# Gate projection of a hybrid attention block: six tiles cut into two pieces of four k-tiles each

## The chip, the cores and the metric

The program runs on one core of one Trainium2 chip. The metric is the device time of one execution, in microseconds (us). The chip's engines are named as in the profile: PE is TensorE's matrix multiply and PEld its weight load, DVE is VectorE, ACT is ScalarE, POOL is GpSimd, SP is SyncE, whose queue issues the DMAs.

## The reference, cut to what matters

One decoder layer is computed for 512 positions and a width of 1024: three attention branches, a gated merge, and a SwiGLU channel mixer. The change touches the gates (`z_a`, the first of three) while branch B, the differential attention, is being computed:

```python
h = rmsnorm(x, g_norm1[l]) * (1 + sc1) + sh1
(a_q, ..., b_q, b_k, b_v, ..., z_a, z_b, z_c) = split_cols(h @ w_in[l], IN_SPLITS)
# branch B, per block of 128 queries and per head:
logits = jnp.einsum('bqhmd,bshmd->bmhqs', qb, k) * ATTN_SCALE + bias
p = jax.nn.softmax(logits, axis=-1)
attn = (p[:, 0] - lam * p[:, 1]).astype(v.dtype)
out = jnp.einsum('bhqs,bshe->bqhe', attn, v)
o_b = rmsnorm(o_b, g_subln[l]) * (1 - lam_init)
merged = (jax.nn.sigmoid(z_a) * (o_a @ w_branch_a[l])
          + jax.nn.sigmoid(z_b) * (o_b @ w_branch_b[l])
          + jax.nn.sigmoid(z_c) * (o_c @ w_branch_c[l]))
```

## The kernel before

Every large projection is computed in split precision: the input and the weights are each cut into a high and a low part, and a k-tile (128 of the 1024 input channels) costs three matmuls of 128x512: high by high (line 846), low by high (847), high by low (848). One output tile of a projection has eight k-tiles and is gathered in one of two PSUM banks, `tile_ps`. Weights come in chunks of 256 columns: SP loads `w_raw` by DMA, ACT rounds it into `w_hi` (line 1419), and DVE subtracts to get `w_lo` (`make_lo`, line 1805). There are two buffers of each.

The middle of the program is a table of steps v = 0 to 87, written out by hand; each engine walks through it in its own fixed order. Steps 64 to 79 are branch B's sixteen (head, block) pairs. Step v has the width 128 x (v mod 4 + 1), so 79 has 512 columns and 76 has 128. The steps 80 to 87 only drain what the sixteen began. Beside the attention work a step can hold a dense piece: a few k-tiles of a projection that has nothing to do with the attention of this step. `dense_at(v)` says which. In this part of the table it is the gate projection: six tiles z0 to z5, from the weight chunks 20 (z0, z1), 21 (z2, z3) and 22 (z4, z5).

In step v of branch B the engines do, each in this order:

- PE: the scores of v, two maps (line 1097), where each map needs the bank that DVE's shift of step v-1 has read; the dense piece, if any; the transposes of the probabilities of v-2 (line 1112), which need DVE's mix of v-2; the products with the values of v-3 (line 1144), which need ACT's copy of the transposes; in steps 73, 77, 81 and 85 the transposes of one head's normed output (line 1175, called the head transposes here), which need DVE's scaling.
- DVE: shift of the first map (add the bias table, take the maximum, line 2014); reciprocal of the sums of v-1 (line 2040), which needs ACT's exponentials; shift of the second map; mix of v-1 (line 2048, first map minus lambda times second), which needs POOL's normalising; then `make_lo` of a weight chunk if `lo_at(v)` names one; then, in steps 71, 75, 79 and 83, one small addition on the mean squares (line 2109); in steps 72, 76, 80 and 84 the scaling of a head's output (line 2119, four blocks); in steps 73, 77, 81 and 85 the low part of it (line 2025).
- ACT: two exponentials (line 1564), a weight chunk's high part if one is due (line 1419), the eviction of a z tile that this step ends (line 1426), the copy of the transposed probabilities (line 1576), and after products that end a head four squares (line 1639).
- POOL: normalising of the second map of v-1 (line 783), then, in steps 71, 75 and 79, the power -1/2 of one head's mean squares (line 729); that of the last head follows step 80.

After step 87 PE goes on at once with the branch A product (`oa_hi`, `oa_lo`; also lines 846 to 848), which needs chunk 23.

The pieces of a z tile have 3, 3 and 2 k-tiles, in three consecutive steps:

```python
Z_STEPS = (66, 69, 72, 76, 80, 84)
for n, v0 in enumerate(Z_STEPS):
    if v0 <= v < v0 + 3:
        return ("z", n), (range(0, 3), range(3, 6), range(6, 8))[v - v0]
```

`chunk_starting_at` names the step in which PE first uses a chunk; ACT makes the high part of the following chunk one step later. `lo_at` names the step in which DVE makes a chunk's low part.

Of the kernel before, what the change touches and what calls it, by code (L numbers as in the profile page):

```python
# [61 lines left out]
MIX_C1, MIX_A, MIX_B, N_MIX = 16, 32, 64, 80  # L62
# [2 lines left out]
SUM_W = 100  # L65
N_DIRECT = (2, 1)
OC_STEPS = (49, 57)
Z_STEPS = (66, 69, 72, 76, 80, 84)
NL_RING, NLB_RING = 4, 7


# [60 lines left out]
def dense_at(v):  # L132

    if v < MIX_A:
        return ("bqk", v // 4), range(2 * (v % 4), 2 * (v % 4) + 2)
    n, part = divmod(v - MIX_A - 2, 4)
    if 0 <= n < 8 and part < 3:
        return ("bv", n), (range(0, 3), range(3, 6), range(6, 8))[part]
    for n, v0 in enumerate(Z_STEPS):
        if v0 <= v < v0 + 3:  # L140
            return ("z", n), (range(0, 3), range(3, 6), range(6, 8))[v - v0]
    return None


def dense_ending_at(v):

    d = dense_at(v)
    return d[0] if d is not None and KT - 1 in d[1] else None


def chunk_starting_at(v):

    return {0: 14, 8: 15, 16: 16, 24: 17, MIX_A + 2: 18, MIX_A + 18: 19, Z_STEPS[0]: 20, Z_STEPS[2]: 21,
            Z_STEPS[4]: 22}.get(v)


def lo_at(v):

    return {2: 15, 10: 16, 18: 17, 26: 18, MIX_A + 5: 19, MIX_A + 21: 20, Z_STEPS[0] + 2: 21, Z_STEPS[2] + 4: 22,
            Z_STEPS[4] + 2: 23}.get(v)  # L160


def attention_tiles():

    names = []
    for v in range(N_STEP):
        if len(qlat_at(v)) == 1:
            names.append(("qlat", qlat_at(v)[0]))
        if dense_at(v) is not None and 0 in dense_at(v)[1]:
            names.append(dense_at(v)[0])  # L170
        for p in products_at(v):
            if uv_after(p) is not None:
                names.append(("uv", uv_after(p)))
        if len(qlat_at(v)) == 2:
            names += [("qlat", h) for h in qlat_at(v)]
        if v in OC_STEPS:
            names.append(("oc", OC_STEPS.index(v)))
        if ob_at(v) is not None:
            names.append(("ob", ob_at(v)))
    return {n: TL_ATT + t for t, n in enumerate(names)}  # L180
# [30 lines left out]
def hybrid_block(nc, a, out):  # L211
# [10 lines left out]
    with ctx:  # L222
# [600 lines left out]
        def _(pe):  # L823
# [354 lines left out]
            def project_z(v):  # L1178

                if chunk_starting_at(v) is not None:  # L1180
                    chunk_ready(chunk_starting_at(v))
                (_, n), kts = dense_at(v)
                project((CH_Z + n // 2) % 2, ATT_TILE["z", n], h_hi, h_lo, [(k, k) for k in kts], n % 2 * P,
                        first=0 in kts, last=KT - 1 in kts)

            def project_b(v):

                if chunk_starting_at(v) is not None:
                    chunk_ready(chunk_starting_at(v))
                (kind, n), kts = dense_at(v)  # L1190
                t = ATT_TILE[kind, n]
                if kind == "bqk":
                    project((CH_BQK + n // 2) % 2, t, h_hi, h_lo, [(k, k) for k in kts], n % 2 * P,
                            first=0 in kts, last=KT - 1 in kts)
                    return
                s, r = (CH_BV + n // 4) % 2, n % 4
                b = tile_start(t) if 0 in kts else t % 2
                for kt in kts:
                    hh, hl = h_hi[:, kt, r * P:(r + 1) * P], h_lo[:, kt, r * P:(r + 1) * P]
                    pe.matmul(tile_ps[b][:, 0:CW], hh, w_hi[s][:, kt, :], start=kt == 0, stop=False)  # L1200
                    pe.matmul(tile_ps[b][:, 0:CW], hh, w_lo[s][:, kt, :], start=False, stop=False)
                    mm = pe.matmul(tile_ps[b][:, 0:CW], hl, w_hi[s][:, kt, :], start=False, stop=kt == KT - 1)
                if KT - 1 in kts:
                    mm.then_inc(tile_made[b], 1)
# [584 lines left out]
        def _(dve):  # L1789
# [239 lines left out]
            for v in range(N_STEP):  # L2029
                if v < N_MIX:  # L2030
                    shift(subs_of(v)[0])
                if v < MIX_B and lo_at(v) is not None:
                    make_lo(lo_at(v))
# [16 lines left out]
                if v >= MIX_B and lo_at(v) is not None:  # L2050
                    make_lo(lo_at(v), kt=4 if lo_at(v) == chunk_z(0) + 3 else KT)
# [346 lines left out]
```

## Time and profile before

| | |
|---|---|
| median of 3 runs | 1005.82 us (1005.34 to 1005.87) |
| profiled execution | 1006.29 us |
| its span, first to last instruction | 1004.5 us |
| PE busy | 987.5 us, 98% of the span |
| DVE busy | 481.5 us, 48% |
| ACT busy | 380.8 us, 38% |
| POOL busy | 98.5 us, 10% |
| granted TensorE clock, mean | 0.999 of full speed |

The profiled execution is 1.8 us longer than its span, which covers what lies before the first and after the last instruction. A timeline row gives the start and the duration of an instruction in us, its engine, line, operation, and what it writes and reads; in brackets stands how long the engine was idle before it and who released it. On PE the ends are modelled and overlap the following instruction, so the distance from one start to the next tells what an instruction costs. A granted clock of 1.00 is the upper of TensorE's two levels, 2.4 GHz.

### The profile page before, as it was taken

What the parts mean: (1) busy time and instruction counts of PE and PEld (TensorE: products, weight loads), DVE (VectorE), ACT (ScalarE), POOL (GpSimd) and SP (SyncE); (2) the same over time, 40 slices, a digit from 0 to 9 for tenths busy, and PEclk for the clock granted to TensorE, in tenths of its full rate; (3) what the DMA queues carried; (4) which work ended last, traced back from release to release, by engine and by line L of the source; (5) the groups of instructions that cost most, each with busy time, mean ns of one, the idle gap of its engine ahead of it and who ended that gap; (6) DMA issues with size and microseconds to landing.
All of it is one profiled execution on the core that took longest, in us unless ns stands there. A gap on an engine that the chain in (4) does not pass through costs nothing.

```text
span 1004.5 us, 12705 instructions
## 1 busy us (share of the span) xinstructions
PE 987.5 (98%) x4925; PEld 805.2 (80%) x4925; DVE 481.5 (48%) x827; ACT 380.8 (38%) x679; POOL 98.5 (10%) x137
## 2 busy tenths in 40 slices
PE   7999999999999999999999999999999999999997
PEld 5778888878877777788788888988888888788886
DVE  4654777833245335663745563743433343331324
ACT  5345422255566666543232232442322322221222
POOL 1500000000054522200000002000000000000401
PEclk9999999999999999999999999999999999999999
DMA  8884226312230201155455642123344434232312
GB/s 330 254 267 143 85 84 177 95 43 84 63 108 22 74 22 33 53 193 195 158 192 198 220 175 84 63 84 104 104 136 151 131 104 147 84 105 84 126 43 84
DMA packets 88164, 123.13 MB, mean 123 GB/s; under 512 B 4825, under 2 KB 69942, under 8 KB 87987
## 3 DMA queue, kind: packets, MB, share of 16 engines
q1 hardware_dynamic: 87442, 115.98, 35.3%
q0 software_dynamic: 528, 6.22, 2.1%
q8 instruction: 32, 0.52, 0.2%
q10 hardware_dynamic: 144, 0.26, 0.1%
q14 instruction: 18, 0.14, 0.0%
HBM read 119.77 MB, written 8.45 MB: 128 GB/s over the span
## 4 chain that ended last, share of the span: by engine, by line
PE 91%; DMA 3%; DVE 2%; ACT 1%; issue 1%; POOL 1%; SPq 0%; POOLq 0%; DVEq 0%; ACTq 0%
PE tile_ps L846 18%; PE tile_ps L848 18%; PE tile_ps L847 18%; DMA w_raw<-in_w_in_dram 2%; PE t_ps L1112 2%; PE s_ps L1094 2%; PE o_ps L1141 2%; PE tile_ps L1295 1%; PE s_ps L1295 1%; PE s_ps L1293 1%; PE t_ps L1295 1%; PE t_ps L1293 1%; PE tile_ps L1294 1%; PE tile_ps L1293 1%; PE s_ps L1294 1%
## 5 line engine op out<-in xcount | busy, mean ns | idle before, releaser
L846 PE MATMUL tile_ps<-h_hi,w_hi 128*128 128x512 f32 x736 | 292.6, 398 | 1.4 <-DVE w_lo L1805 0.8
L848 PE MATMUL tile_ps<-h_hi,w_lo 128*128 128x512 f32 x736 | 287.1, 390 | 0.0
L847 PE MATMUL tile_ps<-h_lo,w_hi 128*128 128x512 f32 x736 | 286.8, 390 | 0.0
L1805 DVE TENSOR_TENSOR w_lo<-w_raw,w_hi 128x2048 fp32r<-128x2048 f32 (+3 forms) x60 | 131.0, 2183 | 161.2 <-ACT w_hi L1419 161.2
L846 PEld LDWEIGHTS tile_ps<-h_hi,w_hi 128*128 128x128 f32 x736 | 138.2, 188 | 38.1 <-issue 8.2
L848 PEld LDWEIGHTS tile_ps<-h_hi,w_lo 128*128 128x128 f32 x736 | 138.1, 188 | 29.3
L847 PEld LDWEIGHTS tile_ps<-h_lo,w_hi 128*128 128x128 f32 x736 | 138.3, 188 | 26.9 <-issue 0.2
L1419 ACT ACTIVATE w_hi<-w_raw 128x2048 fp32r<-128x2048 f32 (+3 forms) x60 | 107.3, 1789 | 42.6 <-DMA w_raw<-in_w_in_dram 10.9
L1802 DVE TENSOR_TENSOR t_lo<-t_raw,t_hi 128x2048 fp32r<-128x2048 f32 (+1 forms) x15 | 32.8, 2183 | 85.6 <-ACT t_hi L1417 85.5
L1564 ACT ACTIVATE nl<-nl,cst 128x256 f32<-128x256 f32 (+3 forms) x81 | 43.0, 531 | 49.3 <-DVE cst L2014 49.2
L1417 ACT ACTIVATE t_hi<-t_raw 128x2048 fp32r<-128x2048 f32 (+1 forms) x15 | 27.0, 1799 | 81.5 <-PE s_ps L1295 53.5
L1752 ACT ACTIVATE f_hi<-f_t 128x512 f32 (+1 forms) x22 | 13.9, 633 | 88.3 <-DVE f_t L2305 88.3
L1576 ACT ACTIVATE pt<-t_ps 128x128 f32<-128x128 f32 (+2 forms) x80 | 32.2, 402 | 28.9 <-PE t_ps L1112 28.2
L769 POOL TENSOR_TENSOR tm<-tab,score 128x256 f32<-128x256 f32 (+2 forms) x24 | 24.3, 1014 | 175.1 <-DVE cst L2014 175.1
L1746 ACT ACTIVATE silu_t<-tile_ps 128x512 f32<-128x512 f32 x22 | 13.0, 597 | 72.0 <-PE tile_ps L848 71.9
L2305 DVE TENSOR_TENSOR f_t<-tile_ps,silu_t 128x512 f32<-128x512 f32 x20 | 13.8, 692 | 54.7 <-PE tile_ps L848 54.7
L804 POOL TENSOR_TENSOR x<-gated,x 128x512 f32<-128x512 f32 x4 | 5.0, 1287 | 297.2 <-DVE gated L2226 297.2
L1112 PEld LDWEIGHTS t_ps<-ident,nl 128*128 128x128 f32 x160 | 20.2, 140 | 12.1 <-issue 4.3
L1112 PE MATMUL t_ps<-ident,nl 128*128 128x128 f32 x160 | 29.6, 275 | 0.0
L2144 DVE SCALAR_TENSOR_TENSOR ada_sum<-ada,cst,ada_sum 128x1024 f32<-128x1024 f32 x21 | 26.9, 1283 | 0.7
L1968 DVE MATCH_REPLACE8 score<-cst,score 128x256 f32<-128x256 f32 (+2 forms) x48 | 26.0, 548 | 0.0
L1960 DVE MAX8 cst<-score 128x8 f32<-128x256 f32 (+2 forms) x48 | 25.2, 556 | 1.4
(404 smaller groups left out, 1679.4 us busy)
## 6 DMA issues: line engine op xcount, KB each, us to landing
w_raw<-in_w_in_dram SPq DMA_DIRECT2D x31, 1024.0 KB, 5.5
w_raw<-in_w_gate_up_dram SPq DMA_DIRECT2D x22, 1024.0 KB, 6.9
ada<-in_w_ada_dram SPq DMA_DIRECT2D x12, 1024.0 KB, 5.5
t_raw<-in_w_down_dram SPq DMA_DIRECT2D x10, 1024.0 KB, 5.0
row_copies<-row_flat POOLq DMA_DIRECT2D x1, 5632.0 KB, 21.6
ada<-in_w_ada_dram SPq DMA_DIRECT2D x8, 640.0 KB, 11.5
ada<-in_w_ada_dram SPq DMA_DIRECT2D x8, 512.0 KB, 4.2
ada<-in_w_ada_dram SPq DMA_DIRECT2D x8, 384.0 KB, 9.9
```

The costliest lines, as they stand in the source:

```text
L846: pe.matmul(dst[0:mw, :], wh, x_hi[:, kx, :], start=start, stop=False)
L847: pe.matmul(dst[0:mw, :], wh, x_lo[:, kx, :], start=False, stop=False)
L848: mm = pe.matmul(dst[0:mw, :], wl, x_hi[:, kx, :], start=False, stop=stop)
L1112: mm = pe.transpose(t_ps[v % 2][:, j * P:(j + 1) * P], src[:, j * P:(j + 1) * P], ident[:])
L1293: pe.matmul(bank[:], x_hi[:, kx, blk], wh[:, kw, :], start=start, stop=False)
L1295: mm = pe.matmul(bank[:], x_lo[:, kx, blk], wh[:, kw, :], start=False, stop=stop)
L1417: act.activation(t_hi[s][:, 0:wide, :], t_raw[s][:, 0:wide, :], ACT.Copy).then_inc(w_hi_made[s], 1)
L1419: hi = nc.scalar.activation(w_hi[s][:, 0:kt, 0:n_cols], w_raw[s][:, 0:kt, 0:n_cols], ACT.Copy)
L1564: act.activation(b, b, ACT.Exp, bias=negmax[:, k:k + 1], scale=-1.0, accum_out=expsum[:, k:k + 1]).then_inc(exped, 1)
L1576: act.activation(pt[v % 2][:, 0:w], t_ps[v % 2][:, 0:w], ACT.Copy).then_inc(pt_ready, 1)
L1802: dve.tensor_tensor(t_lo[s][:, 0:wide, :], t_raw[s][:, 0:wide, :], t_hi[s][:, 0:wide, :].bitcast(F32), ALU.subtract).then_inc(w_split[s], 1)
L1805: dve.tensor_tensor(w_lo[s][:, 0:kt, 0:n_cols], w_raw[s][:, 0:kt, 0:n_cols], w_hi[s][:, 0:kt, 0:n_cols].bitcast(F32), ALU.subtract) \
```

## The change

The six z tiles are cut into two pieces of four k-tiles, and the steps that hold them are written out. Low parts of chunk 22 and 23 are made in steps 75 and 80, where it was 76 and 82.

```diff
-Z_STEPS = (66, 69, 72, 76, 80, 84)
+Z_STEPS = ((66, 67), (69, 70), (71, 73), (74, 75), (78, 79), (82, 83))
@@ dense_at
-    for n, v0 in enumerate(Z_STEPS):
-        if v0 <= v < v0 + 3:
-            return ("z", n), (range(0, 3), range(3, 6), range(6, 8))[v - v0]
+    for n, steps in enumerate(Z_STEPS):
+        if v in steps:
+            part = steps.index(v)
+            return ("z", n), range(4 * part, 4 * part + 4)
@@ chunk_starting_at
-    return {0: 14, 8: 15, 16: 16, 24: 17, MIX_A + 2: 18, MIX_A + 18: 19, Z_STEPS[0]: 20, Z_STEPS[2]: 21,
-            Z_STEPS[4]: 22}.get(v)
+    return {0: 14, 8: 15, 16: 16, 24: 17, MIX_A + 2: 18, MIX_A + 18: 19, Z_STEPS[0][0]: 20, Z_STEPS[2][0]: 21,
+            Z_STEPS[4][0]: 22}.get(v)
@@ lo_at
-    return {2: 15, 10: 16, 18: 17, 26: 18, MIX_A + 5: 19, MIX_A + 21: 20, Z_STEPS[0] + 2: 21, Z_STEPS[2] + 4: 22,
-            Z_STEPS[4] + 2: 23}.get(v)
+    return {2: 15, 10: 16, 18: 17, 26: 18, MIX_A + 5: 19, MIX_A + 21: 20, 68: 21, 75: 22, 80: 23}.get(v)
```

Before, every step from 66 to 86 except 75, 79 and 83 held a piece. After, the steps 68, 72, 76, 77, 80, 81, 84, 85 and 86 hold none; 71, 73, 75, 79 and 83 hold four k-tiles. No engine has more or fewer instructions: 3164 rows on PE, 672 on DVE, 438 on ACT, with POOL and SP unchanged in order too.

On PE, in steps 75 to 77 (scores with `s_ps<-bqk`, transposes with `t_ps<-ident`, products with `o_ps<-bv`), the order was this, with the remaining k-tiles of a piece left out:

```order
L1097 MATMUL s_ps<-bqk 128x512 x2
L1112 MATMUL t_ps<-ident,nl_112 128x128 x2
L1144 MATMUL o_ps<-bv,pt_116 128x128
L1097 MATMUL s_ps<-bqk 128x128 x2
L846 MATMUL tile_ps<-h_hi,w_hi_54 128x512
...
L1112 MATMUL t_ps<-ident,nl_114 128x128 x3
L1144 MATMUL o_ps<-bv,pt_117 128x128 x2
L1097 MATMUL s_ps<-bqk 128x256 x2
```

It is now this, up to the transposes of step 77:

```order
L1097 MATMUL s_ps<-bqk 128x512 x2
L846 MATMUL tile_ps<-h_hi,w_hi_54 128x512
...
L1112 MATMUL t_ps<-ident,nl_112 128x128 x2
L1144 MATMUL o_ps<-bv,pt_116 128x128
L1097 MATMUL s_ps<-bqk 128x128 x2
L1112 MATMUL t_ps<-ident,nl_114 128x128 x3
L1144 MATMUL o_ps<-bv,pt_117 128x128 x2
L1097 MATMUL s_ps<-bqk 128x256 x2
L1112 MATMUL t_ps<-ident,nlb_137 128x128 x4
```

The piece moved from behind the scores of 76 to behind those of 75, and the transposes of 75 (`nlb_137`) now follow the scores of 77 directly, where a piece of three k-tiles stood between them.

On DVE, in the steps 75 and 76, the low part of chunk 22 (`w_lo_55`) passed the small addition, both shifts and the mix of step 75:

```order
 L2048 SCALAR_TENSOR_TENSOR nl_114<-nl_114,cst,nlb_136 128x384
+L1805 TENSOR_TENSOR w_lo_55<-w_raw_51,w_hi_53 128x2048
 L2109 TENSOR_SCALAR cst<-cst 128x4
 L2014 ISA nl_111,cst<-s_ps,tab_129 128x128
...
 L2048 SCALAR_TENSOR_TENSOR nlb_137<-nlb_137,cst,nlb_138 128x512
-L1805 TENSOR_TENSOR w_lo_55<-w_raw_51,w_hi_53 128x2048
 L2119 TENSOR_SCALAR olat<-o_ps,cst 128x128 x4
```

It stands now ahead of the small addition that POOL's power waits for, and ahead of the mix of 75.

On DVE, in step 80, the low part of chunk 23 (`w_lo_56`, half a chunk) moved ahead of the scaling of the third head:

```order
 L2048 SCALAR_TENSOR_TENSOR nlb_138<-nlb_138,cst,nl_111 128x512
+L1805 TENSOR_TENSOR w_lo_56<-w_raw_52,w_hi_54 128x1024
 L2119 TENSOR_SCALAR olat<-o_ps,cst 128x128 x4
 L2025 SCALAR_TENSOR_TENSOR ob_lo<-tile_ps,cst,ob_hi 128x512
-L1805 TENSOR_TENSOR w_lo_56<-w_raw_52,w_hi_54 128x1024
```

The scaling, for which the head transposes of step 81 wait, now comes behind it.

## Rows read from the trace of the kernel before

**Rows 1.** The page, part 1: busy us, share of the span, instructions.

```profile
PE 987.5 (98%) x4925; PEld 805.2 (80%) x4925; DVE 481.5 (48%) x827; ACT 380.8 (38%) x679; POOL 98.5 (10%) x137
```

**Rows 2.** Windows, steps 64 to 87: length, busy us by engine, clock, DMA.

```profile
358.00:429.30 71.30, 70.76 (x389) 52.38 (x388) 38.23 (x126) 42.94 (x134) 14.48 (x21) 1.00 0.15 45
```

**Rows 3.** Timeline of PE: z0's first piece of three k-tiles, step 66.

```profile
365.22 0.50 PE L846 MATMUL tile_ps<-h_hi,w_hi 128*128 128x512 f32 x1
365.55 0.40 PE L847 MATMUL tile_ps<-h_lo,w_hi 128*128 128x512 f32 x1
...
366.02 0.40 PE L846 MATMUL tile_ps<-h_hi,w_hi 128*128 128x512 f32 x1
...
367.39 0.27 PE L1112 MATMUL t_ps<-ident,nlb 128*128 128x128 f32 x1
```

**Rows 4.** Timeline of PE: steps 68 and 69.

```profile
373.85 0.50 PE L846 MATMUL tile_ps<-h_hi,w_hi 128*128 128x512 f32 x1
...
375.35 0.49 PE L1112 MATMUL t_ps<-ident,nl 128*128 128x128 f32 x3
...
376.21 0.70 PE L1097 MATMUL s_ps<-bqk 64*128 64x256 f32 x4
377.08 0.50 PE L846 MATMUL tile_ps<-h_hi,w_hi 128*128 128x512 f32 x1 [0.16 <-ACT z L1426]
```

**Rows 5.** Timeline of DVE: shift of step 68's first map.

```profile
375.33 0.29 DVE L2014 CUSTOM_DVE_ANT_0 nlb<-s_ps,tab 128x128 f32<-128x128 f32 x1
```

**Rows 6.** Timeline of ACT: eviction of z0, and the copy behind it.

```profile
376.45 0.57 ACT L1426 ACTIVATE z<-tile_ps 128x512 f32<-128x512 f32 x1
376.93 0.47 ACT L1576 ACTIVATE pt<-t_ps 128x384 f32<-128x384 f32 x1
```

**Rows 7.** Timeline of PE: steps 75 to 77.

```profile
399.02 1.13 PE L1097 MATMUL s_ps<-bqk 64*128 64x512 f32 x4
...
400.93 0.48 PE L1097 MATMUL s_ps<-bqk 64*128 64x128 f32 x2 [0.19 <-DVE cst L2014]
401.60 0.48 PE L1097 MATMUL s_ps<-bqk 64*128 64x128 f32 x2 [0.19 <-DVE cst L2014]
402.02 0.50 PE L846 MATMUL tile_ps<-h_hi,w_hi 128*128 128x512 f32 x1
...
407.87 0.60 PE L1112 MATMUL t_ps<-ident,nlb 128*128 128x128 f32 x4
```

**Rows 8.** Timeline of DVE: steps 75 and 76.

```profile
402.28 0.17 DVE L2109 TENSOR_SCALAR cst<-cst 128x4 f32<-128x4 f32 x1
...
404.35 0.75 DVE L2048 SCALAR_TENSOR_TENSOR nlb<-nlb,cst,nlb 128x512 f32<-128x512 f32 x1 [1.43 <-POOL nlb L783]
405.02 2.28 DVE L1805 TENSOR_TENSOR w_lo<-w_raw,w_hi 128x2048 fp32r<-128x2048 f32 x1
407.22 1.12 DVE L2119 TENSOR_SCALAR olat<-o_ps,cst 128x128 f32<-128x128 f32 x4
```

**Rows 9.** Timeline of PE: scores of step 79, head transposes of step 81.

```profile
412.97 1.13 PE L1097 MATMUL s_ps<-bqk 64*128 64x512 f32 x4
...
420.59 0.60 PE L1175 MATMUL tile_ps<-ident,olat 128*128 128x128 f32 x4
```

**Rows 10.** Timeline of DVE: scalings of two heads, low part of chunk 23.

```profile
418.98 1.12 DVE L2119 TENSOR_SCALAR olat<-o_ps,cst 128x128 f32<-128x128 f32 x4
...
422.62 1.22 DVE L1805 TENSOR_TENSOR w_lo<-w_raw,w_hi 128x1024 fp32r<-128x1024 f32 x1
...
425.99 1.13 DVE L2119 TENSOR_SCALAR olat<-o_ps,cst 128x128 f32<-128x128 f32 x4 [1.14 <-POOL cst L729]
```

**Rows 11.** Timeline of PE: the last products of branch B, step 82.

```profile
422.42 1.05 PE L1144 MATMUL o_ps<-bv,pt 128*128 128x128 f32 x8
423.27 0.50 PE L846 MATMUL tile_ps<-h_hi,w_hi 128*128 128x512 f32 x1
```

**Rows 12.** Windows at the end of the program, columns as in rows 2.

```profile
998.00:1000.00 2.00, 0.16 (x2) 0.00 (x0) 0.85 (x2) 0.51 (x2) 0.19 (x1) 1.00 0.36 136
1000.00:1002.00 2.00, 0.00 (x0) 0.00 (x0) 0.75 (x1) 0.72 (x1) 0.55 (x1) 1.00 0.00 0
```

## The prediction

> **What bounds the kernel now.** I read the page first: PE is busy for 987.5 us of 1004.5 [rows 1], and nothing else passes half. The program is PE's instructions laid end to end, so the time changes only by what PE pays between them and by what PE waits for. Then I read the windows around the change: in the 71.3 us of steps 64 to 87 PE is busy for 70.76 us [rows 2], so there is hardly a stall to win back, and any stall that the new order brings is added to the end. The list of waits agrees: PE waits in three places of that stretch [rows 4, 7]. Last I followed the timelines of PE, DVE, ACT and POOL step by step. The reader should see there that a step's probabilities travel from PE over DVE, ACT, POOL and DVE back to PE, and that the dense pieces are the work under which PE hides this way. The change takes that cover from some steps and doubles it up in others; PE's total is the same.
>
> **What a piece costs.** The first matmul of a piece is followed after 0.33 us, every other one after about 0.23 [rows 3]: a piece has a start price of 0.10 us. Two further k-tiles take 367.39 - 366.02 = 1.37 us, so 0.69 each; a piece of three is 2.17 us and one of four 2.17 + 0.69 = 2.86 us. Eighteen pieces become twelve. Two of the six starts saved stood behind scores, four behind products or transposes, where the price is much the same; four steps now go from scores straight to transposes, for which I charge 0.05 us each, half the start price, as the transposes also follow the odd-shaped score matmuls. Sum: -6 x 0.10 + 4 x 0.05 = -0.4 us. The bounds are -0.6 (no charge) and -0.2 (the full one).
>
> The Trainium skill bears on that price ("TensorE: Matmul & The Clock Gate", section "Step-by-step: what each phase is for"): it says that PE pulls a weight load ahead of matmuls in flight when row groups don't conflict or when the load goes to the background buffer. By that, a start would cost nothing and the term would be zero, 0.4 us slower than my sum. The trace shows the 0.10 us, so the row decides.
>
> **Waits that go.** In step 69 PE waits for z0's bank: from the scores to z1 it is 377.08 - 376.21 = 0.87 us where those scores alone take 0.63, the 0.70 of the row less its overlap of 0.07 [rows 4], so 0.24 us. z0 will end two steps ahead of z1, and this goes. In step 76 the two score matmuls each wait for a shift of step 75, because step 75 has no piece: 0.19 us, and then 402.02 - 400.93 = 1.09 us for work of 0.42 (from 401.60 to 402.02), so 0.19 + 0.67 = 0.86 us [rows 7]. Step 75 gets a piece, and this goes too. Together -1.1 us.
>
> **Waits that come.** There are four, each the difference between a chain and PE's own work over the same stretch.
>
> - Step 69. It now waits for DVE's first shift of step 68, since step 68 has no piece. That shift ends at 375.62 before [rows 5]. Step 66's longer piece delays all by 0.69, and z0's eviction, now in step 67, takes 0.48 us on ACT [rows 6] ahead of a copy and of the high part of branch A's last head, for which DVE waits ahead of that shift. So 375.62 + 0.69 + 0.48 + 0.06 for the signal = 376.85. PE's work would bring it there at 376.21 + 0.69 + 0.69 for the two longer pieces, - 1.50 for the piece of step 68 (373.85 to 375.35), + 0.05 = 376.14 [rows 4]. Wait: 0.7 us.
> - Step 77. The transposes of step 75 wait for its mix. From the scores of 75 to DVE's small addition it is 402.28 - 399.02 = 3.26 us [rows 7, 8]. The low part of chunk 22, 2.20 us from start to start, now stands before that addition. From the addition over POOL's power and normalising to the end of the mix it is 405.10 - 402.28 = 2.82 us. With 0.05 for the signal the chain is 8.33 us long. PE's own work before was 407.87 - 399.02 = 8.85 us; less the 0.86 of waits, less two pieces of three (4.34), plus one of four (2.86), it is 6.5 us. Wait: 1.8 us. Step 76's and 77's scores are queued ahead and are not late for it; the head transposes of step 77 and everything behind are.
> - Step 80 and 81. From the scores of 79 to the scaling of the third head it is 418.98 - 412.97 = 6.01 us [rows 9, 10]. The half chunk 23, 1.22 less the 0.08 by which DVE's instructions overlap, now stands ahead of it, and the scaling itself takes 1.12: 6.01 + 1.14 + 1.12 + 0.05 = 8.3 us until the head transposes may start. PE's work there was 420.59 - 412.97 = 7.62 us with two pieces of three; with one of four it is 7.62 - 4.34 + 2.86 = 6.15. Wait: 2.2 us, in up to three portions (transposes of 79 and a copy by ACT come late on the way, inside that sum).
> - Step 85. From the start of the last products to the end of the fourth head's scaling it is 427.12 - 422.42 = 4.70 us, over ACT's squares, DVE, POOL and DVE [rows 10, 11]. Two pieces of z5 (six k-tiles) covered it; now the products take 0.85 and one piece 2.86, 3.71 in all. Wait: 4.75 - 3.71 = 1.0 us.
>
> The sum is 0.7 + 1.8 + 2.2 + 1.0 = 5.7 us that come, -1.1 that go, -0.4 for starts: **+4.2 us**.
>
> **What costs nothing.** The evictions of z2 to z4 move by a step or two; they are under 0.6 us on ACT [rows 6], and between a tile's end and the next tile in that bank PE has at least the transposes, products and scores of a step. The high parts of chunks 22 and 23 are made one and two steps earlier, still steps ahead of their low parts. The DMA queue only waits on DVE's low parts and shifts in this stretch, and chunk 24 is asked for once the low part of 22 is made, a dozen steps before its use. After step 87 PE continues with 24 matmuls of the branch A product on chunk 23, 24 x 0.23 = 5.5 us, which is ready long before. Under it lie ACT's and DVE's work for the next tiles, as before; z5's eviction comes off that stretch, which gives at most 0.05 us. Later stages are paced by PE, which waits for nothing there, so the delay reaches the end unchanged.
>
> **How the sum stands.** On the profiled execution it gives a span of 1008.7 and 1010.5 us in all; this execution is 0.47 us over the median of the runs. On the median: 1005.82 + 4.2 = 1010.0 us.
>
> **The rivals.**
>
> - *The chains are shorter than charged.* Each was put together from distances that contain waits of DVE for PE, for example that DVE reached the addition of step 75 late since step 74's and 75's shifts came close together. If DVE runs further ahead, the two middle waits are halved: 2.0 us less, 1008.0. Against: the scores that start both chains are the trigger in any order, and what follows them has no slack in the rows. 8%.
> - *The cover was not needed* (the other side). If the transposes and head transposes find their data in time, as they do in every step of the trace now, only the terms with a minus stay: 1005.8 - 1.5 = 1004.3 us. The deciding point is whether the four waits together stay under 1.5 us. For it: none of the four waits exists in the trace. Against: for each the chain is over the cover by 0.7 to 2.2 us. 5%, within 0.2% of before; going beyond that, 2%, would need a saving in the starts of over twice the row.
> - *The clock falls.* The pauses bring PE's activity down around steps 76 to 81. If the granted clock fell to 1.2 GHz for the length of one piece, 2.86 us would double: 1012.9 us. Against: at the end of the program PE has hardly worked from 998 to 1002 us and the granted clock in these rows is still 1.00, that is 2.4 GHz [rows 12]. 4%. The Trainium skill ("TensorE: Matmul & The Clock Gate", section "What's actually happening") says that the clock's default is the throttled level and that it goes back there when PE is idle; the rows show a longer idle stretch without a fall, so the page does not change the sum.
> - *The change doesn't do what it says.* The order on each engine excludes this: the pieces stand where the table puts them.
>
> **How the numbers follow.** The forecast has 81%. Its own range, from +2.8 (every wait 0.3 smaller) to +5.2 (each 0.2 larger, starts at -0.2), is 1008.6 to 1011.0. Down to 1007.6 the range takes in the first rival; the upper end is 1011.2. What is left out is the second rival, the clock, and tails. A measurement of this kernel tells 0.2% (2.0 us) from no change. Slower by more: the forecast, the clock, and half of the first rival, 0.88 with tails. Within: the other half and the second rival, 0.10. Faster: 0.02.
>
> **What would show it.** PE's busy time in the stretch should stay and its length grow by 4 us. The list of waits should have PE waiting for the mix (line 2048) before the transposes of step 75, for the scaling (line 2119) before the head transposes of steps 81 and 85, and for a shift (line 2014) before the scores of 69; the waits for z and in step 76 should be gone. If the low part of chunk 22 is not between the mix of 74 and the addition in time, or the gaps sum to under 3 us, the chains were misjudged; if matmul distances rise above 0.23 us, it is the clock.

## The result, and the profile after

The changed kernel takes 1012.66 us in the median of 4 runs (1011.89 to 1013.77), the kernel before 1005.85 us; the ratio is 1.0063 with a 95% interval of 1.005 to 1.0075. It is slower, as forecast, but by 6.8 us where 4.2 were forecast, and outside the range, whose upper end was 1011.2. The profiled execution took 1011.89 us, with a span of 1009.7.

The page, part 1, of the changed kernel; [rows 1] is the same line of before:

```profile
PE 988.9 (98%) x4925; PEld 805.8 (80%) x4925; DVE 481.5 (48%) x827; ACT 381.6 (38%) x679; POOL 99.0 (10%) x137
```

PE's busy time has grown by 1.4 us although it runs the same 4925 instructions. That is a first sign that something else than waiting was added.

The start of the program differs from execution to execution (z0's first matmul begins at 365.22 us before, at 363.67 after, with nothing changed ahead of it), so I compare one stretch in all runs: from the first matmul of z0 to the first of the branch A product, called **the stretch** below. It is read from one profiled execution of each kernel. It was 429.32 - 365.22 = 64.10 us long and is 434.14 - 363.67 = 70.47 us now, 6.37 more. In windows of exactly these bounds (length, busy us by engine, clock, DMA), the kernel before:

```profile
365.22:429.32 64.10, 63.56 (x343) 47.58 (x343) 35.88 (x114) 38.33 (x119) 13.35 (x19) 1.00 0.15 46
```

and the changed one:

```profile
363.67:434.14 70.47, 65.70 (x344) 49.17 (x343) 35.34 (x113) 39.01 (x119) 13.41 (x19) 0.98 0.14 42
```

PE stands still for 4.8 us of it instead of 0.5, is busy for 2.1 us more (65.70 against 63.56), and the granted clock is 0.98 on average instead of 1.00. The waits, in the timeline of PE of the changed kernel; the two waits of [rows 7] and the one of [rows 4] are gone:

```profile
375.30 0.97 PE L1097 MATMUL s_ps<-bqk 64*128 64x256 f32 x4 [0.65 <-DVE cst L2014]
...
409.14 0.99 PE L1112 MATMUL t_ps<-ident,nlb 128*128 128x128 f32 x4 [1.49 <-DVE nlb L2048]
...
422.43 0.71 PE L1144 MATMUL o_ps<-bv,pt 128*128 128x128 f32 x4 [0.33 <-ACT pt L1576]
...
423.42 0.66 PE L1112 MATMUL t_ps<-ident,nlb 128*128 128x128 f32 x4 [0.27 <-DVE nlb L2048]
...
425.68 0.63 PE L1175 MATMUL tile_ps<-ident,olat 128*128 128x128 f32 x4 [0.94 <-DVE olat L2119]
...
433.75 0.63 PE L1175 MATMUL tile_ps<-ident,olat 128*128 128x128 f32 x4 [1.06 <-DVE olat L2119]
```

They stand at the four places that the prediction named: the scores of step 69, the transposes of 75, the steps 80 and 81, the head transposes of 85. What it had put at 4% is there too. The windows of two microseconds around the second wait, same columns; the third number from the end is the clock:

```profile
406.00:408.00 2.00, 1.62 (x10) 1.03 (x8) 0.90 (x7) 1.25 (x5) 1.49 (x2) 1.00 0.15 35
408.00:410.00 2.00, 0.85 (x5) 0.86 (x6) 1.66 (x5) 0.00 (x0) 0.30 (x1) 0.83 1.02 358
410.00:412.00 2.00, 2.00 (x11) 1.86 (x10) 1.22 (x7) 1.50 (x5) 0.45 (x1) 0.50 0.00 0
412.00:414.00 2.00, 2.00 (x9) 1.13 (x8) 0.97 (x2) 0.76 (x2) 0.00 (x0) 0.82 0.00 0
```

0.50 is the lower of TensorE's levels, 1.2 GHz. PE had worked on small matmuls since 404.7 us and waited for 1.5 us up to 409.14. The clock fell when PE was already at work again: a mean of 0.83 over 2 us is 0.68 us at the lower level, so since 409.3. By the 0.82 of the last window it was back at about 412.7. Under the lowered clock lay most of the transposes of 75 (the row of 409.14 above) and, behind them, the products and head transposes of step 77 and the scores of 78:

```profile
409.93 1.49 PE L1144 MATMUL o_ps<-bv,pt 128*128 128x128 f32 x6
411.21 1.06 PE L1175 MATMUL tile_ps<-ident,olat 128*128 128x128 f32 x4
412.20 1.16 PE L1097 MATMUL s_ps<-bqk 64*128 64x384 f32 x4
413.29 0.50 PE L846 MATMUL tile_ps<-h_hi,w_hi 128*128 128x512 f32 x1
```

That is 4.15 us from the transposes (409.14) to the piece (413.29). The same instructions took from 407.87 [rows 7] to 410.35 in the kernel before, 2.48 us. By these rows the lowered clock cost 1.7 us.

### The profile page after: what moved, and what is told of

It reads as the page before. It is cut to its first block, busy times and chain, and to the rows that moved or that the text cites. A ratio compares the mean times of both kernels' runs of the same rounds, so it can differ in the third digit from the quotient of the medians.

```text
span 1009.7 us, 12705 instructions
## 1 busy us (share of the span) xinstructions
PE 988.9 (98%) x4925; PEld 805.8 (80%) x4925; DVE 481.5 (48%) x827; ACT 381.6 (38%) x679; POOL 99.0 (10%) x137
## 4 chain that ended last, share of the span: by engine, by line
PE 90%; DMA 3%; DVE 2%; issue 2%; ACT 1%; POOL 1%; SPq 0%; POOLq 0%; DVEq 0%; ACTq 0%
PE tile_ps L846 18%; PE tile_ps L848 18%; PE tile_ps L847 17%; DMA w_raw<-in_w_in_dram 2%; PE t_ps L1112 2%; PE s_ps L1094 2%; PE o_ps L1141 2%; PE tile_ps L1294 1%; PE tile_ps L1293 1%; PE s_ps L1294 1%; PE s_ps L1293 1%; PE t_ps L1294 1%; PE t_ps L1293 1%; PE tile_ps L1295 1%; PE s_ps L1295 1%
```

## The experiments

Ten kernels were run. All stretches stand in one table, with what was forecast for each. "Clock falls" is about the stretch. Each ratio is to runs of the kernel before on the same chip, whose medians were 1005.85 us for the changed kernel, 1006.37 for the edits of one place and the six fill matmuls, 1005.94 for the two runs that take the change apart ("both low parts"), and 1006.03 for the rest.

| run | stretch, us | forecast | clock falls | median, us | ratio (95%) |
|---|---|---|---|---|---|
| before | 64.10 | | no | 1005.85 | |
| changed | 70.47 | 68.3 | yes | 1012.66 | 1.0063 (1.005 to 1.0075) |
| low part of 22 in step 73 | 67.70 | 67.5 | no | 1010.31 | 1.004 (1.0026 to 1.0054) |
| six fill matmuls in step 77 | 68.93 | 68.8 | no | 1011.13 | 1.0047 (1.003 to 1.0063) |
| three fill matmuls | 68.88 | 68.9 | no | 1012.36, one run | |
| low part of 23 in step 82 | 69.33 | 69.4 | yes | 1011.21 | 1.006 (1.0036 to 1.0084) |
| z5 in steps 83, 84 | 69.18 | 69.4 | yes | 1012.15 | 1.0061 (1.0044 to 1.0078) |
| the three edits at once | 65.25 | 65.5 | no | 1007.36 | 1.0012 (1.0003 to 1.0022) |
| changed, both low parts back | 70.28 | 70.1 | yes | 1012.43 | 1.0062 (1.0045 to 1.0079) |
| before, both low parts moved | 65.03 | 64.8 | no | 1007.66 | 1.0013 (1.0003 to 1.0023) |
| fours, placed anew | 63.50 | 63.3 | no | 1005.62 | 0.9997 (0.9988 to 1.0006) |
| mixed pieces | 62.80 | 62.4 | no | 1005.14 | 0.9991 (0.9982 to 1.0) |

**The low part of chunk 22 off the chain.**

```diff
-    return {..., 68: 21, 75: 22, 80: 23}.get(v)
+    return {..., 68: 21, 73: 22, 80: 23}.get(v)
```

> One number of the changed kernel differs: DVE makes the low part of chunk 22 in step 73 instead of 75, off the chain from the scores of 75 to the mix of 75. My theory (the low part is 2.2 us of that chain, and the pause it makes lets the clock fall): the wait of 1.49 us before the transposes of step 75 goes, the head transposes of step 77 then wait a little for the scaling, and the granted clock stays at 1.00 from 408 to 414 us. From the first z0 matmul to the first branch A product it is 70.47 us in the changed kernel; it becomes 70.5 - 1.3 - 1.7 = 67.5 us, the median about 1009.7 us. Rival (the clock falls because the steps 76 and 77 hold only small matmuls, wait or not): only 1.3 us go, 69.2 us, and the clock still falls. Second rival (the wait comes from the missing cover alone and another link is late next): the wait stays within 0.5 us of what it was, 70 us.

The wait before the transposes of 75 in that run:

```profile
409.48 0.66 PE L1112 MATMUL t_ps<-ident,nlb 128*128 128x128 f32 x4 [0.56 <-DVE nlb L2048]
```

The stretch fell by 2.8 us for 2.2 us of DVE's work moved by two steps: 0.9 us of the wait, and the clock, which stayed at 1.00. The wait did not go as far as I expected; 0.56 us are left, and the head transposes of step 77 did not wait at all. What holds the mix of 75 (408.68 us in that run) is now another chain. DVE's shift of step 76 stands ahead of the reciprocal of step 75 and waits for PE's scores of 76:

```profile
407.39 0.29 DVE L2014 CUSTOM_DVE_ANT_0 nl<-s_ps,tab 128x128 f32<-128x128 f32 x1 [1.54 <-PE s_ps L1097]
```

POOL's normalising had been idle for 0.92 us when that reciprocal released it at 407.87; the power was long done. So a low part of 2.2 us is worth only 0.9 us of wait there.

**Is it the pause that lowers the clock?** The pause can be filled without changing its cause:

```diff
+                if v == 77:
+                    b = tile_start(ATT_TILE["ob", 1])
+                    for _ in range(6):
+                        pe.matmul(tile_ps[b][:], h_hi[:, 0, 0:P], h_hi[:, 0, :], start=True, stop=True)
                 for t in transposes_at(v):
```

> The changed kernel with six more matmuls of 128x512 on PE in step 77, ahead of the transposes of step 75; their product is thrown away, so nothing that is computed changes. At 0.23 us each they fill 1.4 us of PE's wait of 1.49 us. My theory (the pause of PE is what makes the clock fall): the order's wait stays as time, now filled, the granted clock stays at 1.00, and the stretch from the first z0 matmul to the first branch A product goes from 70.47 to 68.8 us, the median to about 1011.0. Rival (the clock falls for another reason, such as the small matmuls of steps 76 and 77): the clock still falls and the stretch stays at 70.5 us or grows by what the fill costs.

In that run everything stands 2.1 us later (z0 begins at 365.75 us), so these windows hold the fill, the transposes of 75 and the work behind them; the clock is 1.00 in the rest of the stretch too:

```profile
410.00:412.00 2.00, 2.00 (x13) 1.50 (x12) 1.55 (x5) 0.03 (x1) 0.41 (x1) 1.00 1.03 363
412.00:414.00 2.00, 2.00 (x15) 1.29 (x14) 1.33 (x7) 1.39 (x5) 0.45 (x1) 1.00 0.06 18
```

PE does more and the stretch is 1.5 us shorter (68.93 against 70.47). (The added lines shift the line numbers below them by 4 in these two runs.) With three fill matmuls instead of six:

> As the run with six fill matmuls in step 77, but with three: they take 0.7 us of PE's wait of 1.49 us, and leave 0.8 us of it. If the length of the pause decides about the clock, it stays at 1.00 with 0.8 us as it did with 0.56 us (low part of chunk 22 in step 73), and the stretch is 68.9 us. If any pause after the small matmuls of steps 76 and 77 is enough, the clock falls for 3 us or so, and the stretch is 70.5 us.

```profile
411.71 0.66 PE L1112 MATMUL t_ps<-ident,nlb 128*128 128x128 f32 x4 [0.60 <-DVE nlb L2052]
```

A wait of 0.60 us remains, the clock stays at 1.00, the stretch is the same 68.9 us. (Its one time, 1012.36 us, holds a late start: z0 begins at 366.23 us against 363.67 in the changed kernel.) The fills add work to PE as well as shorten its pause; the low part of 22 in step 73 shortened the pause and added nothing to PE. So the small matmuls of steps 76 and 77 do not lower the clock by themselves, and 0.56 us of pause right behind them don't either; 1.49 us at this place did in all three runs that had it.

The length of the pause alone does not decide, though. The kernel before with its low parts moved (below) has a longer wait far ahead of the stretch, behind matmuls that are mostly of 128x512:

```profile
81.80 0.50 PE L845 MATMUL tile_ps<-h_hi,w_hi 128*128 128x512 f32 x1 [1.73 <-DVE w_lo L1804]
```

The clock is 1.00 there and in every window behind it up to the end of the stretch. The Trainium skill's rule ("TensorE: Matmul & The Clock Gate", section "What's actually happening"), that the clock falls back when PE has been idle, fits the fall behind 1.49 us; by itself it does not tell that wait from this one of 1.73 us.

**The low part of chunk 23 behind the scaling.** In `lo_at`, `80: 23` became `82: 23`.

> One number of the changed kernel differs: DVE makes the low part of chunk 23 in step 82 again, behind the scaling of the third head. My theory (its 1.14 us lie on the chain from the scores of 79 to the head transposes of step 81): PE's wait there of 0.94 us goes, and the stretch from the first z0 matmul to the first branch A product shrinks by 1.1 us to 69.4, the clock falling near 409 us as before; median about 1011.6. Rival (the wait is for ACT's copies and the mix, which come late in step 80 too): less than 0.5 us goes.

The stretch fell by 1.14 us, the half chunk's time on DVE, and the wait in step 81 left the list. The copy (0.31 us) and the mix (0.26) of step 80 stayed, so these are a part of their own, as the rival had it, but a small one.

**z5 behind the last products.** In `Z_STEPS`, `(82, 83)` became `(83, 84)`.

> One pair of numbers of the changed kernel differs: z5's two pieces stand in steps 83 and 84 instead of 82 and 83, so both follow the last products. My theory (the head transposes of step 85 come 4.75 us after the start of the last products, and PE has only 3.7 us of work between): that work becomes 0.85 + 5.7 = 6.6 us, the wait of 1.06 us goes, and the stretch from the first z0 matmul to the first branch A product shrinks by 1.0 us to 69.4; median about 1011.6. Rival (the last products then wait longer, for ACT's copy, and take the wait over): the stretch stays within 0.3 us.

The wait of 1.06 us left the list, and the stretch fell by 1.3 us. The clock fell in this run too, but long before: from the head transposes of step 81 to the branch A product it is 434.14 - 425.68 = 8.46 us in the changed kernel and 433.47 - 426.27 = 7.20 here, with the clock at 1.00 in both. So the gain of 1.3 us lies all behind the fall.

**All three at once.**

> The changed kernel with three of the earlier edits at once: low part of chunk 22 in step 73, of chunk 23 in step 82, z5 in steps 83 and 84. My theory (the waits are separate chains, so their gains add): the stretch from the first z0 matmul to the first branch A product, 64.10 us in the kernel before and 70.47 in the changed one, becomes 70.47 - 2.77 - 1.14 - 1.05 = 65.5 us, the clock stays at 1.00, and the median is about 1.4 us over the kernel before. What is left is the wait in step 69 (0.65 us and slower score matmuls), about 0.5 us for the mix of 75, and 0.6 us for a copy and the mix in step 80. Rival (the chains overlap, and removing one uncovers the next): 66.5 us or more.

65.25 us: the gains add up (1.14 + 1.29 + 2.77 = 5.20 apart, 5.22 together). The waits are separate chains and not one that hides another.

**Only the low parts, only the pieces.** The two halves of the change were taken apart: the kernel before with `lo_at` of the change,

> The kernel before, with only the low parts moved as in the change: chunk 22 in step 75, chunk 23 in step 80; the pieces stay 3, 3 and 2. My theory (a low part costs only where the pieces no longer cover the chain): no wait before the transposes of step 75, since the chain of 8.33 us stays under the 8.85 us that PE takes there; in step 81 the chain of 8.3 us meets 7.62 us of work, so the head transposes wait 0.7 us; the stretch from the first z0 matmul to the first branch A product goes from 64.10 to 64.8 us and the clock stays at 1.00. Rival (the low parts alone bring most of the loss): waits of 1.5 to 2 us in steps 77 and 81, 67 us or more.

```profile
420.90 0.63 PE L1174 MATMUL tile_ps<-ident,olat 128*128 128x128 f32 x4 [0.67 <-DVE olat L2118]
```

and the changed kernel with `76: 22, 82: 23`:

> The changed kernel with both low parts back in steps 76 and 82, so that only the pieces are new. My theory (the pieces carry the loss): the wait for the mix of 75 shrinks to about 0.6 us, but the low part of chunk 22 now stands ahead of the second head's scaling, for which the head transposes of step 77 wait about 2 us, long enough for the clock to fall; the wait in step 81 is gone; the stretch is 70.1 us against 70.47. Rival (the low parts carry the loss): the stretch falls to 66 us or less.

```profile
409.25 0.66 PE L1112 MATMUL t_ps<-ident,nlb 128*128 128x128 f32 x4 [0.57 <-DVE nlb L2048]
...
412.58 0.63 PE L1175 MATMUL tile_ps<-ident,olat 128*128 128x128 f32 x4 [2.00 <-DVE olat L2119]
```

(In the first of these two, the line numbers are one lower.) The low parts alone cost 0.9 us, at the place and of the size forecast; ahead of the transposes of step 75, where the low part of 22 cost most in the changed kernel, there is no wait at all under the old pieces. The pieces alone cost 6.2 us: with the low part of 22 behind the mix, it only stands in front of the scaling instead, the wait is 2.00 us long, and the clock falls after it (0.85, 0.50 and 0.80 in the three windows of 2 us from 412 on). So the pieces' new places bring the loss whether or not the low parts move with them; what they cost depends on what stands on the uncovered chains, for with two low parts and z5 elsewhere it is 1.15 us (65.25 against 64.10).

**Is it the size of four or the place?** Pieces of four at other steps:

```diff
-Z_STEPS = ((66, 67), (69, 70), (71, 73), (74, 75), (78, 79), (82, 83))
+Z_STEPS = ((66, 67), (68, 69), (71, 73), (76, 78), (80, 81), (83, 84))
-    return {..., 68: 21, 75: 22, 80: 23}.get(v)
+    return {..., 68: 21, 73: 22, 82: 23}.get(v)
```

> The changed kernel's pieces of four, placed where the chains want cover: steps (66, 67), (68, 69), (71, 73), (76, 78), (80, 81), (83, 84), low parts in 73 and 82. My theory (pieces of four are fine, and only their places cost): all waits but some 0.5 us in steps 75 and 76 are gone, six starts are saved, the stretch is 63.3 us against 64.10 in the kernel before, the median 0.8 us below it. Rival (a piece of four is itself too coarse for the steps, so waits of 2 us stay wherever it goes): 65 us or more.

The stretch is 63.50 us, 0.6 below the kernel before, and PE's list of waits has nothing in it; only the scores of step 76 take 0.82 us to the piece behind them where they take 0.42 to the transposes in the changed kernel. With pieces of mixed sizes:

```diff
+Z_STEPS = ((66, 67, 68), (69, 70, 71), (72, 73, 74), (75, 76, 77, 78), (80, 81), (84,))
+Z_KTS = ((2, 3, 3), (3, 3, 2), (3, 3, 2), (2, 2, 2, 2), (5, 3), (8,))
...
+            k0 = sum(Z_KTS[n][:part])
+            return ("z", n), range(k0, k0 + Z_KTS[n][part])
...
+    return {..., 68: 21, 77: 22, 82: 23}.get(v)
```

> Pieces of different sizes: z0 2, 3, 3 in 66 to 68; z1 and z2 3, 3, 2 as in the kernel before; z3 four pieces of two in 75 to 78; z4 5 and 3 in 80 and 81; z5 whole in 84; low parts of chunks 22 and 23 in 77 and 82. My theory: no wait of PE is left between step 66 and the branch A product, and the stretch is 62.4 us against 64.10 in the kernel before (1.1 us of waits and some starts less), the median 1.7 us below it. Rival (the small pieces of two leave the mix or the scaling late in steps 75 to 78): a wait of 0.5 to 1 us before the head transposes of step 77, and 63.3 us.

The window of the stretch in that run:

```profile
364.27:427.07 62.80, 62.80 (x344) 47.15 (x343) 35.35 (x113) 38.00 (x119) 13.34 (x19) 1.00 0.14 44
```

PE is busy for the whole of it. 1.3 us less than before is 0.13%. The ratio of 0.9991 points that way, but its interval ends at 1.0; the fours placed anew are 0.9997 with 1 well inside. In the stretch both are faster than the kernel before; in the time of the program only the mixed pieces come near to being told from it.

## Why the prediction was wrong, point by point

- **PE's chain is the time, its total the same**: right as to the waits. With the trace of the changed kernel read, the stretch of each of the ten experiments was forecast to 0.4 us from sums of rows.
- **Waits that go, -1.1 us**: right. The waits for z0's bank and in step 76 are gone from the list.
- **Step 69, 0.7 us**: the wait is 0.65 us. Mis-sized by 0.27: the two score matmuls there take 376.20 - 375.30 = 0.90 us to the piece instead of 0.63, since the second waits for its own shift, which ends 0.28 us after the first, and no longer overlaps the first. I had charged this in step 76 [rows 7] and forgot it here.
- **Step 77, 1.8 us**: the chain from the scores of 75 to the transposes was forecast at 8.33 us and is 409.14 - 400.79 = 8.35. The wait that the trace shows is smaller, 1.49 us, as part of it lies in the scores of 77 ahead of it.
- **Steps 80 and 81, 2.2 us**: the chain was forecast at 8.3 and is 425.68 - 417.27 = 8.41 us, in three portions as said. These sum to 1.54 us (0.33, 0.27, 0.94) and not to 2.2, because a wait is counted from the modelled end of the row before it (0.49 us for the transposes at 421.62) and my work from start to start (0.32 for the like at 375.35 in the kernel before). The length of the whole is what tells.
- **Step 85, 1.0 us**: 1.06 us, the chain 433.75 - 428.90 = 4.85 for 4.75.
- **The sum, +4.2**: with the pause filled, so that the clock stays up, the stretch is 4.8 us longer than before (68.93 and 68.88 against 64.10). 0.27 of the missing 0.6 is step 69, and 0.2 are the chains of 81 and 85. Another 0.09 are the scores of 78, which have no piece in the step before them: 413.88 - 412.95 = 0.93 us to the piece in the run with six fills, 410.35 - 409.51 = 0.84 before. Under 0.1 is left. In the median that run is 4.8 us over its runs of before (1011.13 against 1006.37), which lies inside the forecast's range.
- **The clock, 4%**: this is the step that failed. The term for the clock was put at nothing, and it measured 1.5 to 1.7 us. I took the rows at the end of the program [rows 12], where PE has stopped and the clock is still 1.00, as proof that a pause does not bring the clock down. The idle stretch that I called one without a fall ends in a fall, in the very next row of the same view:

```profile
1002.00:1004.00 2.00, 0.00 (x0) 0.00 (x0) 0.00 (x0) 0.00 (x0) 0.00 (x0) 0.59 0.70 262
```

  So the trace of before held the behaviour, some 4 us after PE's last matmul (at the latest 998.2 us; by the mean of 0.59 the fall came near 1002.4), and my reading stopped one row short of it. The rows of [rows 12] show that the clock falls late, not that it does not fall. In the changed kernel, too, it was at 1.00 throughout the pause and fell when PE was back at work. The sign that I had named for the clock, matmul distances above 0.23 us, would have missed it there: it was over before the first 128x512 matmul of step 78.
- **The clock's price, 2.86 us for a piece of four**: too high. The lowered clock met the small matmuls of step 77 and the scores of 78 and cost 1.7 us by the rows, 1.5 by the run with the fill. That this rival's 1012.9 us is so near the measured 1012.66 is luck: its price was over by 1.2 us, the sum that it was added to was short by 0.5 us, and 0.4 us of the difference of the medians lie outside the stretch.
- **Chains shorter than charged, 8%**: did not happen; the chains are 0.02 to 0.11 us longer than forecast.
- **The other side** (the cover was not needed, 5%): did not happen at these places. Without waits, and shorter than before, the stretch is only with the pieces at other steps.

The medians differ by 6.8 us and the stretches by 6.4; the execution profiled of the changed kernel was the fastest of its four.

## What to carry to other kernels

Where an engine with no slack hides other engines' chains under filler work, look at the filler's place before its grain. Here pieces of four k-tiles took 70.47 us at one set of places and 63.50 at another, with two low parts moved along. For every consumer, add up the chain from its trigger and compare it with what the bound engine does in between, and count on the chain whatever shares an in-order engine with it. A pause of TensorE may cost more than its length. Before a new order is dismissed or taken, check the waits against the granted clock in the windows behind them, and read on until the clock or the trace ends before calling a pause harmless.

## What the runs showed of the hardware that was not expected

- A wait of PE of 1.49 us behind 2.9 us of small matmuls was followed by a granted clock of 0.50 where it had been 1.00, in each of the three kernels that had it, and so was one of 2.00 us, which followed a wait of 0.57. The fall came after PE was back at work, 0.2 us after in the changed kernel and 0.7, 1.0 and 0.8 in the runs with 23 in step 82, z5 in 83 and 84, and both low parts back (estimates from the means of the 2 us windows). Waits of 0.56 and 0.60 us at the same place did not. Nor did three waits of 0.33, 0.27 and 0.94 us within 4 us, in steps 80 and 81 of the changed kernel, though PE was busy for only 1.06 of 2 us in one window there:

```profile
424.00:426.00 2.00, 1.06 (x10) 0.90 (x9) 1.54 (x5) 0.60 (x1) 0.00 (x0) 1.00 0.21 22
```

  Nor did the wait of 1.06 us in step 85 of that kernel, or the one of 1.73 us shown above. Why some waits lower it and others do not stays open.
- At the end of the program the clock stayed at 1.00 for some 4 us after PE's last matmul and then fell to 0.50 (1003 to 1004 us in the kernel before).
- Six matmuls whose result is thrown away made the program faster in the stretch by 1.5 us.
